# Two transformer blocks on one core: where norm sums stand on TensorE, who squares the first and last norm's tiles, and ScalarE's order in the woven mixers

## The reference

```python
for l in range(2):
    x = x + 0.5 * swiglu(rms_norm_2(x, ffn1_norm[l]), ffn1_w_in[l], ffn1_w_out[l])
    h = rms_norm_2(x, mix_norm[l]);  z = h @ w_mix_in[l]
    o = concat(rms(o_mla), rms(o_swa), rms(o_na))      # three attentions over parts of z, one norm per group
    x = x + o @ w_mix_out[l]
    x = x + mem_xattn(rms_norm_2(x, mem_norm_x[l]), mem, ...)
    x = x + 0.5 * swiglu(rms_norm_2(x, ffn2_norm[l]), ffn2_w_in[l], ffn2_w_out[l])
    x = rms_norm_2(x, block_norm[l])
# rms_norm_2(x, g) = x * rsqrt(mean(x * x, over the 1024 features) + EPS) * g
```

## Time and profile before

| | us |
|---|---|
| median of 3 runs (3094.51 to 3096.02) | 3094.77 |
| the profiled execution | 3099.33 |
| its span | 3097.1 |
| TensorE busy | 2940.3 (95%) |
| VectorE, ScalarE, GpSimd busy | 1464.5, 1088.3, 237.5 |

### The profile page before, as it was taken

How to read it: one execution, slowest core, us unless ns; L and a number is a source line. 1 busy time by engine, 2 the same in 40 slices (tenths; PEclk the granted TensorE clock), 3 DMA queues, 4 the chain that set the end, 5 groups by cost and what they waited for, 6 DMA issues and landing times.

```text
span 3097.1 us, 36136 instructions
## 1 busy us (share of the span) xinstructions
PE 2940.3 (95%) x13424; PEld 2329.6 (75%) x13424; DVE 1464.5 (47%) x2032; ACT 1088.3 (35%) x1771; POOL 237.5 (8%) x176
## 2 busy tenths in 40 slices
PE   8878999889899999998999999999999998999998
PEld 5667777668678888567768888888886677778886
DVE  5653257733354433555444443544434555354432
ACT  4512234434222322555433322322223645332221
POOL 0000000000110012100220002200021001120012
PEclk9989899989999999999999999999999999999999
DMA  3100221112322233011212232222322110222232
GB/s 120 61 14 8 72 77 60 48 38 93 122 82 95 95 107 141 19 51 35 74 50 95 95 105 97 84 100 95 105 89 102 35 50 33 69 88 95 95 110 74
DMA packets 68360, 238.03 MB, mean 77 GB/s; under 512 B 10272, under 2 KB 12448, under 8 KB 67616
## 3 DMA queue, kind: packets, MB, share of 16 engines
q1 hardware_dynamic: 66240, 227.87, 22.2%
q10 hardware_dynamic: 2016, 8.77, 0.7%
HBM read 234.51 MB, written 2.10 MB: 76 GB/s over the span
## 4 chain that ended last, share of the span: by engine, by line
PE 65%; DVE 3%; ACT 2%; issue 1%; DMA 0%; POOLq 0%; DVEq 0%; POOL 0%; ACTq 0%; SPq 0%; PEldq 0%
PE bank L373 18%; PE bank L375 18%; PE bank L374 18%; PE bank L833 3%; PE bank L859 2%; PE bank L635 2%; PE bank L845 2%; PE bank L645 1%; PE bank L1452 1%; ACT L_probs L903 1%; PE bank L1429 0%; DVE L_scores L951 0%; DVE L_h_lo L468 0%; DVE L_weight_ring_low L367 0%; ACT L_squares L1544 0%
## 5 line engine op out<-in xcount | busy, mean ns | idle before, releaser
L373 PE MATMUL bank<-L_h_hi,L_w_hi 128*128 128x512 f32 x1776 | 707.8, 399 | 22.5 <-DVE L_h_lo L468 13.3
L375 PE MATMUL bank<-L_h_hi,L_weight_ring_low 128*128 128x512 f32 x1776 | 693.5, 390 | 0.0
L374 PE MATMUL bank<-L_h_lo,L_w_hi 128*128 128x512 f32 x1776 | 693.3, 390 | 0.0
L361 ACT CAST L_w_hi<-L_weight_ring 128x1024 fp32r<-128x1024 f32 (+2 forms) x292 | 326.1, 1117 | 918.3 <-PE bank L375 910.1
L367 DVE TENSOR_TENSOR L_weight_ring_low<-L_weight_ring,L_w_hi 128x1024 fp32r<-128x1024 f32 (+2 forms) x292 | 394.6, 1351 | 382.6 <-ACT L_w_hi L361 382.4
L373 PEld LDWEIGHTS bank<-L_h_hi,L_w_hi 128*128 128x128 f32 x1776 | 334.6, 188 | 104.1 <-issue 16.5
L374 PEld LDWEIGHTS bank<-L_h_lo,L_w_hi 128*128 128x128 f32 x1776 | 335.0, 189 | 74.9 <-issue 6.8
L375 PEld LDWEIGHTS bank<-L_h_hi,L_weight_ring_low 128*128 128x128 f32 x1776 | 334.5, 188 | 70.1
L375 PE MATMUL bank<-L_act_hi,L_weight_ring_low 128*128 128x512 f32 x704 | 274.0, 389 | 0.0
L373 PE MATMUL bank<-L_act_hi,L_w_hi 128*128 128x512 f32 x704 | 273.9, 389 | 0.0
L374 PE MATMUL bank<-L_act_lo,L_w_hi 128*128 128x512 f32 x704 | 273.9, 389 | 0.0
(11 more groups left out here) (304 smaller groups left out, 3901.8 us busy)
## 6 DMA issues: line engine op xcount, KB each, us to landing
L_weight_ring<-ffn_in SPq DMA_DIRECT2D x176, 512.0 KB, 3.2
L_weight_ring<-ffn_out SPq DMA_DIRECT2D x64, 704.0 KB, 4.0
B_weight_ring<-w_sqk SPq DMA_DIRECT2D x24, 512.0 KB, 3.2
B_weight_ring<-w_dn SPq DMA_DIRECT2D x16, 512.0 KB, 3.3
B_weight_ring<-w_gate SPq DMA_DIRECT2D x16, 512.0 KB, 3.2
L_weight_ring<-w_sna_qk SPq DMA_DIRECT2D x16, 512.0 KB, 3.2
L_weight_ring<-w_mix_out SPq DMA_DIRECT2D x16, 512.0 KB, 3.2
B_weight_ring<-w_sv SPq DMA_DIRECT2D x12, 512.0 KB, 3.3
```

Of the source, the lines that this page charges most:

```text
L361: e.copy(hv.high(at)[:, 0:width], sh.ring[:, at % RING, 0:width]).then_inc(hv.w_hi_done, 1)
L373: e.matmul(out, a_hi, b_hi, start=start, stop=False)
L374: e.matmul(out, a_hi, b_lo, start=False, stop=False)
L375: return e.matmul(out, a_lo, b_hi, start=False, stop=stop)
```

## The change

1. In a feed-forward stage's first turn the norm's sum moves from behind the third strip to behind its tile k = 3 (the first stage of layer 1 keeps its place).
2. At the entry ScalarE and VectorE make the halves of tiles 0 to 2, then of strip 0, of tiles 3 to 7, then of strip 1. ScalarE then squares the eight tiles into eight places, and GpSimd only adds seven of them.
3. In the mixers ScalarE walks a list of its own. A "norm" turn is now one square (the fourth also makes Ln and Exp). Group 0's four stand inside job 22's turn, between the finish of job 21 and the begin of job 22; group 1's stand one by one between units, and its "norm_used" and the two rows behind it come two units later on every engine.
4. At the end GpSimd sums seven tiles; ScalarE squares the eighth, and TensorE adds both in one bank by two matmuls. ScalarE no longer waits for the last two strips ahead of its table load.

```diff
-def norm_pool(e, seen, sh, src, width=T, wait_x=True, first=False, also=None):
+def norm_pool(e, seen, sh, src, width=T, wait_x=True, first=False, also=None, tiles=KT):
...
-    for k in range(KT):
+    for k in range(tiles):
...
-        e.tensor_tensor(acc, acc, sq, ALU.add).then_inc(sh.sq_step if k < KT - 1 else sh.sq_summed, 1)
+        e.tensor_tensor(acc, acc, sq, ALU.add).then_inc(sh.sq_step if k < tiles - 1 else sh.sq_summed, 1)
...
                     mm = halves_mm(e, sh.banks[2 * j + part][:, :], hv, s, k, hv.h_hi[:, k, :],
                                    hv.h_lo[:, k, :], k == 0, k == KT - 1)
-                mm.then_inc(sh.strip_done, 1)
-                if first and (j, part) == ((1, 0) if more_norm is None else (0, 1)):
-                    norm_pe(e, seen, sh)
-                    if more_norm is not None:
-                        more_norm()
+                    if k == KT - 1:
+                        mm.then_inc(sh.strip_done, 1)
+                    if first and (j, part, k) == ((1, 0, 3) if more_norm is None else (0, 1, KT - 1)):
+                        norm_pe(e, seen, sh)
+                        if more_norm is not None:
+                            more_norm()
...
-            e.wait_ge(sh.strip_done, seen.ready(sh.strip_done))
+            strips = seen.ready(sh.strip_done)
+            if i < 2 * KT - 2 or next_width is not None:
+                e.wait_ge(sh.strip_done, strips)
...
+def jobs_act_steps(e, seen, sh, jb, jobs, hv=None, at=0, early=(), sum_banks=None, pause=False):
...
+                if pause and j in early:
+                    yield
...
+        entry_squares = [sh.sq_sum[:, :]] + [flat[:, i * T:(i + 1) * T] for i in range(11, 18)]
...
-            mix_turns += ["unit"] + ["split"] * (i >= 10) + ["unit"] + {17: ["norm"], 18: ["norm_used"]}.get(i, []) + ["job"]
+            mix_turns += ["unit"] + ["split"] * (i >= 10) + ["unit"] + {18: ["norm_used"]}.get(i, []) + ["job"]
         mix_turns += ["unit", "unit", "row"] * 4
-        mix_turns += ["unit"] * 4 + ["norm"] + ["unit"] * 2 + ["norm_used"] + ["unit"] * 2 + ["row"]
-        mix_turns += ["unit"] * 2 + ["row"] + ["unit"] * 6
+        mix_turns += ["unit"] * 4 + ["norm", "unit"] * 3 + ["norm", "unit", "norm_used", "unit", "unit", "row"]
+        mix_turns += ["unit"] * 2 + ["row"] + ["unit"] * 4
+        act_turns, job = [], 0
+        for name in mix_turns:
+            act_turns.append(name)
+            if name == "job":
+                if job in sums_first:
+                    act_turns += ["norm"] * (4 if job == 22 else 0) + ["job"]
+                job += 1
...
+                e.wait_ge(sh.sq_summed, seen.ready(sh.sq_summed))
+                e.matmul(banks[7][:, :], ones, sh.sq_sum[:, :], start=True, stop=False)
+                e.wait_ge(last_sq, 1)
+                e.matmul(banks[7][:, :], ones, sh.sq[:, 0, :], start=False, stop=True).then_inc(sh.norm_mm, 1)
...
-                        split_strip_act(e, seen, sh, hv, 0, W_IN)
                         e.wait_ge(gains_in, 16 * LAYERS)
                         for k in range(KT):
                             h_high_act(e, sh, g("ffn1"), hv.h_hi_done, hv.h_hi[:, k, :], k)
                             if k == 2:
-                                split_strip_act(e, seen, sh, hv, 1, W_IN)
+                                split_strip_act(e, seen, sh, hv, 0, W_IN)
+                        split_strip_act(e, seen, sh, hv, 1, W_IN)
+                        for k in range(KT):
+                            e.activation(entry_squares[k], xT[:, k, :], ACT.Square).then_inc(entry_sq, 1)
...
+                                if t < TT - 1:
+                                    yield
...
-                    take_turns(mix_turns, job=jobs_act_steps(e, seen, sh, jb, mix_jobs, hv, at0 + sna_at - 2 * MLA_HEADS, sums_first),
+                    take_turns(act_turns, job=jobs_act_steps(e, seen, sh, jb, mix_jobs, hv, at0 + sna_at - 2 * MLA_HEADS, sums_first,
+                                                              pause=True),
                                unit=attn_act_steps(e, seen, sh, at_, mix_units), norm=norms, row=rows, split=splits_act())
-                    next(norms)
+                    for t in range(TT):
+                        next(norms)
...
+                e.wait_ge(sh.x_done, 2 + LAYERS * X_PER)
+                e.activation(sh.sq[:, 0, :], xT[:, KT - 1, :], ACT.Square).then_inc(last_sq, 1)
...
-                        split_strip_dve(e, seen, sh, hv, 0, W_IN)
                         for k in range(KT):
                             h_low_dve(e, seen, sh, hv, g("ffn1"), k)
                             if k == 2:
-                                split_strip_dve(e, seen, sh, hv, 1, W_IN)
+                                split_strip_dve(e, seen, sh, hv, 0, W_IN)
+                        split_strip_dve(e, seen, sh, hv, 1, W_IN)
...
-                        norm_pool(e, seen, sh, xT, wait_x=False, first=True)
+                        for k in range(1, KT):
+                            e.wait_ge(entry_sq, k + 1)
+                            if k > 1:
+                                e.wait_ge(entry_add, k - 1)
+                            e.tensor_tensor(sh.sq_sum[:, :], sh.sq_sum[:, :], entry_squares[k], ALU.add)\
+                                .then_inc(entry_add if k < KT - 1 else sh.sq_summed, 1)
...
-                    norm_pool(e, seen, sh, xT, also=raw_add if layer < LAYERS - 1 else None)
+                    if layer < LAYERS - 1:
+                        norm_pool(e, seen, sh, xT, also=raw_add)
+                    else:
+                        norm_pool(e, seen, sh, xT, tiles=KT - 1)
```

More of the change, by code:

```diff
@@ L654, in jobs_pe @@
     return at + sum(len(job["parts"]) for job in jobs)
-def jobs_act_steps(e, seen, sh, jb, jobs, hv=None, at=0, early=(), sum_banks=None):
+def jobs_act_steps(e, seen, sh, jb, jobs, hv=None, at=0, early=(), sum_banks=None, pause=False):
     sum_banks = jb.sum_banks if sum_banks is None else sum_banks
@@ L1147, in layers_program @@
         x_normed = sc.sem("residual_normalised")
+        last_sq = sc.sem("last_tile_squared")
+        entry_sq = sc.sem("entry_squared")
+        entry_add = sc.sem("entry_squares_added")
         v_rows = [jb.rs[:, 1, :], jb.g[:, 0, :], jb.g[:, 1, :]]
```

## The result

Measured: 3067.4 us (median of 4, 3065.4 to 3072.3) against 3095.4, 28.0 us less; ratio 0.991 (95% interval 0.9893 to 0.9927). Beside three other kernels, the changed one was timed again: 3068.5 against 3098.0, ratio 0.9905 (0.989 to 0.992), 29.4 us. Forecast: 3070.0, or 25.4 under that 3095.4.

The account below looks back on a forecast made before the run. TensorE, busy 2940.3 of 3097.1 us, was taken as the bound, so only its idle or slow time could be won. Five steps summed to 24.8 us, taking the median from 3094.77 to 3070.0, range 3064.5 to 3075.5.

Parts of the forecast that it names:

- Step 1: Entry: without GpSimd beside it VectorE's halves run at short durations, so the fifth strip starts 8.5 us sooner.
- 2, two more stages: Second feed-forward stage of layers 0 and 1: norm's sum inside the third strip removes TensorE's idle spell; 3.5 us.
- Step 3: Mixers, job 22: Ln and Exp ahead of norm work remove TensorE's idle spell and slow stretch; 8.4 us, both layers.
- Step 4: Mixers, group 1's norm: squares one by one fit ScalarE's idle spells and no longer delay a copy; 2.7 us.
- 5, the end: End of kernel: ScalarE squares the last tile and TensorE's second matmul adds it, without waiting for GpSimd; 1.7 us.
- rival A2: Mixers and memory attention: two or more of eight lower-clock stretches go, 3066.5 down to 3064 us; chance 0.12.

Follow-up runs that it names:

- the entry kernel: The kernel before with only the entry's new order of halves and ScalarE's squares, norm's sum still behind the third strip; 3095.1 against 3097.9, again 3093.3 against 3098.0.

## Why the prediction was right

Each of its places can be read as the change of TensorE's lag behind the old trace, matmul by matmul:

| step | forecast, us | in the trace |
|---|---|---|
| 1, entry up to the fifth strip | 8.5 | 8.6 |
| 2, two more stages | 3.5 | 3.6 |
| 3, job 22, two layers | 8.4 | 4.6 + 4.4 |
| 4, group 1, two layers | 2.7 | 1.6 + 1.5 |
| 5, the end | 1.7 | 1.8 |
| sum | 24.8 | 26.1 |

Step 1: h_lo at 0.75 us, TensorE's start 9.8 us behind the last matmul (9.4 by the working, 10.0 before), strip 0 over 17.0 us behind it, the strip's first part at the lower clock, as said. (The working's 9.5 slow matmuls in 4.2 us don't follow from its own 0.41 us each, which gives 10.2; that is worth 0.2 us.) One microsecond of the agreement is luck: the working takes the slow stretch from the old trace, and the changed kernel's trace happened to have it at about the same place; with the late one (35.2) the step is 7.6. The run with GpSimd squaring shows the cause: the long durations of the earlier trace rows came from GpSimd working beside VectorE, not from VectorE's own work. The order of the halves brings nothing here: with the old one TensorE starts 1.3 us sooner, the sum is late and the fifth strip comes 0.5 later, and the rest of edit 2 is the gain. The idle time ahead of the fifth strip is edit 1's: 36.0 without, 34.2 with it (both with the early slow stretch).

The margin of the sum was 0.4 us, where the prediction had at least 0.5 by the rows and about nothing by the rule of the Trainium skill (page "SBUF — State Buffer", section "Who interferes with whom"). Seven adds took 11.11 us. The prediction priced each at 1.26 to 1.61 with nothing between them; the trace has five of 1.3 us, one of 1.7 and one of 2.08, and 0.14 us from each to the next. The rule has the mechanism right. The split of strip 2 is shown from 855.40 for 2.35 us, twice its 1.23 with GpSimd idle, and so ends about its own length behind the add that was running when it came; the next add, from 856.82, ends 1.15 us behind the split. In the kernel with strip 0 first two adds on the chain were 2.1 us long beside such a split, and the sum was late.

Step 3 was too small by 0.3 a layer; the spell of 2.85 us went whole, and the slow stretch behind it with it. Step 4's pieces fell into what had been ScalarE's idle spells, the fourth with Ln and Exp too, and nothing was lost to the later scaling. Where the prediction speaks of "edits 3 to 5" and of "edits 1, 2 and 5" it means its steps; the change has four edits.

What the sum doesn't hold: the profiled execution gained 34.0 us, 7.9 more than the steps. 1.5 of it came ahead of the entry. Between 1200 and 3000 us there were ten stretches at PEclk 0.50 before and five after, so three fewer besides the two of job 22, at 1.5 each some 4.5. The rest, 1.9, is not placed. This is rival A2's mechanism; its time, 3064 to 3066.5, is 1 us under the median of 3067.4. In the medians the surplus is smaller than in this one execution (28.0 and 29.4 us less, against 26.1 for the steps). The place of a given stretch is not a property of the change, since the same kernel shows other ones in another execution. Their number may be: in the ten traces of kernels with edit 3 it is five to nine between 1200 and 3000 us (five in both of the changed kernel), in the four without it nine or ten. Job 22's two explain a part of that; that the change is behind the others too is not shown.

The parts measured alone add up: 14.6 + 4.7 + 9.5 = 28.8, against 29.4 for the whole, timed beside the last two (26.9 with the entry's first median, 2.8). What stays open is the entry's part. Its traces show 6.8 and 5.9 us, its medians 2.8 and 4.7. The traces show nothing given back behind the fifth strip (2215.4 and 2216.5 us to the end, 2215.7 before), so scatter is the likelier reason; ten and eleven times that spread over 11 and 9 us don't prove it.

## What to carry to other kernels

When VectorE's operations between SBUF tiles take twice their least duration, look first at what GpSimd runs beside them; moving half of GpSimd's work to an idle ScalarE was worth more than any order (6.1 us against nothing). Work that nobody waits for yet (a norm's squares) belongs behind the instruction that releases the next wait, not ahead of it, and in pieces where the engine has idle spells. A sum whose result is needed late may stand in the middle of an accumulation, but its own inputs then need a margin: measure it, as the next improvement elsewhere may eat it.

## What the runs showed of the hardware

- TensorE's granted clock fell to its lower level behind idle spells of 1.75 to 2.9 us, behind two of 1.1 and 0.7 us close together, and a few times behind one of 1.0 to 1.4, in some executions and not in others of the same kernel: the spell of 1.84 us near 1274 us has such a stretch behind it in the first trace of the entry kernel and none in the second. Where one trace has a stretch and the other none, the lag changes by 1.5 to 1.7 us. Four runs of one kernel spread over 1.4 to 12 us. For steps of 1 to 2 us the distance inside a trace is the better measure, if the slow stretches in it lie alike.
- A table load on ScalarE cost 1.28 us, with 0.02 us ahead of it and 0.01 behind, also between two activations.
- GpSimd's adds of 128x512 took 1.30 us alone and 2.07 to 2.10 beside a split on VectorE; VectorE's h_lo took 0.75 alone and 1.5 to 1.8 beside GpSimd, its split 1.23 and up to 2.35. Both sides pay.
